# Block products in the down projections: five weight slots of eleven worked as seven products with summed weights in place of eight

## The chip, the cores and the metric

One core of one Trainium2 chip. The number reported is the device time of one execution in microseconds. The core has four compute engines that run their own instruction queues and meet at semaphores: TensorE (PE), VectorE (DVE), ScalarE (ACT) and GpSimd (POOL). SyncE (SP) issues the DMAs.

## What is computed

Two transformer-like blocks over 256 tokens of width 1024, all in float32. Four times in it stands a gated feed-forward of this form, with the inner width F = 2816:

```python
def swiglu_ffn(h, w13, w2):
    gate, up = jnp.split(h @ w13, 2, axis=-1)
    return (jax.nn.silu(gate) * up) @ w2      # (256, 2816) @ (2816, 1024)

x = x + 0.5 * swiglu_ffn(rms_norm(x, ffn1_norm[l]), ffn1_w13[l], ffn1_w2[l])   # ffn 0; ffn 1 alike
h = h + swiglu(rms_norm_2(h, ln_ffn[i]), ffn_w_in[i], ffn_w_out[i])            # ffn 2 and 3
```

Between them stand a convolution and attention mixer (after ffn 0), a gated delta rule mixer (after ffn 1, with the first block's final norm ahead of it), a gated embedding and a stick-breaking attention (after ffn 2), and a gated embedding at the end (after ffn 3). The change is in the products with `w2` and `ffn_w_out`, the down projections `down0` to `down3`.

## The kernel before

**Precision.** TensorE works in its rounded float32. Each float32 matrix is split into a rounded part and the rest (`whi`, `wlo` for weights, `hThi`, `hTlo` for the hidden state, `xThi`, `xTlo` for the input of other products), and each product is three matmuls, hi by hi, hi by lo and lo by hi (`passes`, L1717 to L1719). One such matmul has 128 rows of contraction, 128 tokens and 512 columns.

**The ring of weights.** All weights stream through one list of slots of 128x2048 float32 (1 MB). SP loads slot w into `raw[w % 4]` once slot w-4 is wholly split (L422, L423). ACT rounds it into `whi[w % 4]` once TensorE has used slot w-4 (`split`, L457). VectorE subtracts, `wlo = raw - whi` (L1112, or in two halves, L1109 and L1112, for a few slots). TensorE waits for `w_lo` and counts up `w_used` when it is done with a slot. ACT and VectorE each go through their queues in program order; `split(n)` means "go on through slot n-1", so a written order decides what else stands between two splits.

**A down projection** is 11 slots (`wide`). A slot holds two blocks of 128 rows of the weight and its 1024 columns, and is worked for both tiles of 128 tokens: 2 token tiles by 2 row blocks by 2 halves of 512 columns, 8 block products, 24 matmuls. The sums stay in four PSUM banks (6, 7, 2, 3). The first seven slots are taken one after the other; the last four are first worked for token tile 0 and then for tile 1, so that tile 0 comes out early. Ahead of the last quarter of tile 1 stand the transposes of the next stage's first token tile (`turn_T`, L1751).

**What follows a down.** VectorE adds the banks to the residual `X` (`residual`, L1158), ACT sums squares (L481), GpSimd takes the root (L1001, L1002), VectorE scales (L1127), TensorE transposes (L1751), ACT and VectorE split the result into `xThi`, `xTlo` (L488, L1135), and the next stage's products begin. VectorE splits the next slots of the ring in between.

**What goes into a down.** The hidden state of each of the 11 blocks is transposed in 32x32 pieces by VectorE (L1176), written to memory and read back by DMA (L406, L413), and split by ACT and VectorE (`hidden_hi` L513, `hidden_lo` L1168). Blocks 8, 9 and 10 are split while the down runs.

## Time and profile before

| | |
|---|---|
| median of 3 runs | 1212.18 us (1209.71 to 1213.11) |
| the profiled execution | 1209.79 us, span 1208.1 us |
| granted TensorE clock | 1.00 of full in every slice |
| busy: PE, DVE, ACT, POOL | 1191.5, 786.5, 610.5, 80.1 us |
| first down projection | 133.25 to 193.99 us of the span |

The busy time of an engine is over the whole span. Matmuls are pipelined and their records overlap, so the distance between starts is their pace, not the duration of one. The remaining 1.7 us of the profiled time lie around the span.

### The profile page before, as it was taken

Reading aid. Unit: us, or ns where it says so; the run is one execution under the profiler, and the core shown is the slowest. Engines: PE = TensorE matmul, PEld = TensorE weight load, DVE = VectorE, ACT = ScalarE, POOL = GpSimd, SP = SyncE. Lnnn points to the kernel's source line nnn. Section 1 sums busy time; section 2 is a strip of 40 time slices with the busy share of each in tenths; the row PEclk is TensorE's granted clock in tenths of the full one; section 3 lists DMA queues with packets and bytes.
Section 4 is the critical chain, followed back from the end, with each engine's and each line's share of the span. In section 5 each row is a group of like instructions: output and inputs, shape, how many; then the busy total and the mean of one; then the engine's idle time right before and its main releaser. Section 6 shows DMA issues by size and latency. Waiting matters only on the chain.

```text
span 1208.1 us, 16080 instructions
## 1 busy us (share of the span) xinstructions
PE 1191.5 (99%) x6352; PEld 1011.9 (84%) x6352; DVE 786.5 (65%) x941; ACT 610.5 (51%) x770; POOL 80.1 (7%) x151
## 2 busy tenths in 40 slices
PE   8999999999999999999999999999999999999998
PEld 6888888988888888899898888888888888888886
DVE  4766547997665654788877756553688666565545
ACT  5544426565544443565644544543556755445333
POOL 1000003001000000400002000000114000000000
PEclk9999999999999999999999999999999999999999
DMA  8987764552588775545203688686355347877630
GB/s 272 318 279 250 236 217 147 160 192 59 177 271 244 243 243 175 193 157 174 88 1 105 193 274 256 218 255 211 136 206 202 131 129 233 259 257 230 227 136 36
DMA packets 174547, 235.32 MB, mean 195 GB/s; under 512 B 13993, under 2 KB 131849, under 8 KB 174473
## 3 DMA queue, kind: packets, MB, share of 16 engines
q1 hardware_dynamic: 174472, 234.30, 60.0%
q8 instruction: 50, 0.82, 0.3%
q14 instruction: 25, 0.20, 0.0%
HBM read 221.67 MB, written 12.58 MB: 194 GB/s over the span
## 4 chain that ended last, share of the span: by engine, by line
PE 93%; DVE 4%; ACT 1%; POOL 1%; DMA 0%; issue 0%; SPq 0%; DVEq 0%; ACTq 0%
PE bank L1717 28%; PE bank L1718 28%; PE bank L1719 28%; PE bank L1751 1%; PE bank L2146 1%; PE bank L2163 1%; PE bank L2171 1%; DMA raw<-in_ffn_w_dram 0%; PE bank L1970 0%; DVE xs L1523 0%; DVE bv L1378 0%; PE bank L2268 0%; DVE xs L1127 0%; PE bank L2290 0%; PE bank L1957 0%
## 5 line engine op out<-in xcount | busy, mean ns | idle before, releaser
L1112 DVE TENSOR_TENSOR wlo<-raw,whi 128x2048 fp32r<-128x2048 f32 (+1 forms) x190 | 415.9, 2194 | 236.4 <-ACT whi L457 236.4
L457 ACT ACTIVATE whi<-raw 128x2048 fp32r<-128x2048 f32 x190 | 362.9, 1914 | 227.2 <-PE bank L1719 218.4
L1717 PE MATMUL bank<-whi,xThi 128*128 128x512 f32 x1024 | 401.8, 392 | 0.9 <-DVE xTlo L1659 0.8
L1719 PE MATMUL bank<-whi,xTlo 128*128 128x512 f32 x1024 | 398.9, 390 | 0.0
L1718 PE MATMUL bank<-wlo,xThi 128*128 128x512 f32 x1024 | 398.5, 389 | 0.0
L1717 PEld LDWEIGHTS bank<-whi,xThi 128*128 128x128 f32 x1024 | 192.3, 188 | 41.4 <-DVE xTlo L1659 1.4
L1719 PEld LDWEIGHTS bank<-whi,xTlo 128*128 128x128 f32 x1024 | 192.2, 188 | 40.3
L1718 PEld LDWEIGHTS bank<-wlo,xThi 128*128 128x128 f32 x1024 | 192.3, 188 | 38.8
L1717 PE MATMUL bank<-whi,hThi 128*128 128x512 f32 x352 | 137.3, 390 | 0.0
L1719 PE MATMUL bank<-whi,hTlo 128*128 128x512 f32 x352 | 137.0, 389 | 0.0
L1718 PE MATMUL bank<-wlo,hThi 128*128 128x512 f32 x352 | 136.9, 389 | 0.0
L541 ACT ACTIVATE hnat<-bank 128x256 f32<-128x256 f32 x88 | 33.6, 384 | 122.3 <-PE bank L1719 122.3
L1717 PE MATMUL bank<-xThi,whi 128*128 128x256 f32 x288 | 82.3, 286 | 0.0
L1718 PE MATMUL bank<-xTlo,whi 128*128 128x256 f32 x288 | 81.5, 283 | 0.0
L1719 PE MATMUL bank<-xThi,wlo 128*128 128x256 f32 x288 | 81.4, 283 | 0.0
L1719 PEld LDWEIGHTS bank<-whi,hTlo 128*128 128x128 f32 x352 | 66.1, 188 | 13.7
L1717 PEld LDWEIGHTS bank<-whi,hThi 128*128 128x128 f32 x352 | 66.1, 188 | 13.7
L1718 PEld LDWEIGHTS bank<-wlo,hThi 128*128 128x128 f32 x352 | 66.1, 188 | 13.5
L1001 POOL TENSOR_SCALAR meansq<-sumsq 128x1 f32<-128x1 f32 x16 | 12.4, 773 | 841.0 <-ACT xs L481 665.1
L1193 DVE TENSOR_TENSOR hnat<-hnat,bank 128x256 f32<-128x256 f32 x88 | 36.7, 417 | 45.8 <-ACT hnat L541 45.8
L1717 PEld LDWEIGHTS bank<-xThi,whi 128*128 128x128 f32 x288 | 55.2, 192 | 1.3 <-issue 0.8
L1718 PEld LDWEIGHTS bank<-xTlo,whi 128*128 128x128 f32 x288 | 55.2, 192 | 0.0
(425 smaller groups left out, 1064.3 us busy)
## 6 DMA issues: line engine op xcount, KB each, us to landing
raw<-in_ffn_w_dram SPq DMA_DIRECT2D x176, 256.0 KB, 4.5
raw<-in_ffn_w_in_dram SPq DMA_DIRECT2D x176, 256.0 KB, 4.0
raw<-in_ffn_w_dram SPq DMA_DIRECT2D x22, 1024.0 KB, 5.3
raw<-in_ffn_w_out_dram SPq DMA_DIRECT2D x22, 1024.0 KB, 5.4
raw<-in_gdn_w_in_dram SPq DMA_DIRECT2D x16, 1024.0 KB, 5.5
hidden<-hblk SPq DMA_DIRECT2D x44, 256.0 KB, 5.1
hraw<-hidden SPq DMA_DIRECT2D x176, 64.0 KB, 3.3
raw<-in_ple_w_gate_dram SPq DMA_DIRECT2D x8, 1024.0 KB, 5.0
```

The costliest lines, as they stand in the source:

```text
L457: act.activation(whi[w % SPLIT][:], raw[w % RAW][:], ACT.Copy).then_inc(w_hi, 1)
L541: act.activation(hnat[:, j % 2, t, :], bank[2 * (j % 2) + t][:, 0:256], ACT.Silu).then_inc(sem("ffn_silu"), 1)
L1001: step(pool.tensor_scalar(meansq[:, c], sumsq[:, 2 * n + t, 0:1], sumsq[:, 2 * n + t, 1:2], EPS, ALU.add, ALU.add))
L1112: dve.tensor_tensor(wlo[w % SPLIT][:, c], raw[w % RAW][:, c], whi[w % SPLIT][:, c].bitcast(F32), ALU.subtract).then_inc(w_lo, 1)
L1193: dve.tensor_tensor(hnat[:, j % 2, t, :], hnat[:, j % 2, t, :], bank[2 * (j % 2) + t][:, 256:512], ALU.mult).then_inc(sem("ffn_h"), 1)
L1717: pe.matmul(psum, lhs[0], rhs[0], start=start, stop=False, skip_group_check=True)
L1718: pe.matmul(psum, lhs[0], rhs[1], start=False, stop=False, skip_group_check=True)
L1719: return pe.matmul(psum, lhs[1], rhs[0], start=False, stop=stop, skip_group_check=True)
L1751: ins = pe.transpose(bank[4 + b][:, k * P:(k + 1) * P], xs[:, t, (4 * b + k) * P:(4 * b + k + 1) * P], ident[:])
L2146: ins = pe.matmul(bank[q][:, h * P:(h + 1) * P], A_[q][:, h, :], T[q][:, h, :], start=True, stop=True)
L2163: ins = pe.matmul(bank[q][:, c], U[q][:, h, :], Y[q][:, c], start=True, stop=True)
L2171: ins = pe.matmul(psum[:, h * P:(h + 1) * P], lhs(h), rhs(h), start=True, stop=True)
```

## The change

Five slots of each down (row block pairs 1, 2, 4, 5 and 6) are worked as 2x2 block matrices by seven products in place of eight. For that each of them takes two places of the ring: its own, with the quarters b0, b1 (first row block, left and right half of the columns), b2, b3 (second row block), 128x512 each, and behind it a place without a DMA, which holds four sums of quarters: GpSimd computes t0 = b0-b1 and t1 = b0-b2 in one instruction (`first_combined`), VectorE t2 = b2-t0 and then t3 = b3-t2, which waits for it (`combine`). Of the first place only three quarters are rounded and split; the second is rounded and split whole. On the side of the hidden state GpSimd adds hi and lo back together (`h_all`) and forms four sums S1 to S4 of it (`hidden_sums`), which ACT rounds (`sums_hi`) and VectorE splits (`sums_lo`) into the buffers of `xThi` and `xTlo`, free while a down runs. Each of the five takes 21 matmuls in place of 24. The products go to seven banks in all; four of these hold parts that belong to more than one output quarter, and after the last split of a down VectorE adds them to `X` with 4+3+2+2 instructions (`shared_sums`), ahead of the adds of `residual`. A down is now 16 places of the ring, of which five have no DMA. `wide` passes over the second place of each pair and calls `seven` for the first.

The diff, cut; what is left out are the names of buffers and the calls that pass `pair_at`:

```diff
+
+    def stream_down(name, w):
+        first[name] = len(slots)
+        v = w.rearrange("(k p) n -> p k n", p=P)
+        for s in range(KF // 2):
+            slots.append([(("rows", 2), v[:, 2 * s:2 * s + 2, :])])
+            if s in SEVEN:
+                slots.append([])
+
     stream_gate_up("up0", a["ffn1_w13"][0])
-    stream_wide("down0", a["ffn1_w2"][0])
+    stream_down("down0", a["ffn1_w2"][0])
     stream_pairs("mix", a["w_in"][0])
...
 
 
     WIDE = ["down0", "mix_out", "down1", "gdn_out", "down2", "ple_g0", "sb_out", "down3", "ple_g1"]
-    wide_slots = {n: (KF if n[:4] == "down" else KD) // 2 for n in WIDE}
+    wide_slots = {n: KF // 2 + len(SEVEN) if n[:4] == "down" else KD // 2 for n in WIDE}
+    pair_at = {s + sum(x < s for x in SEVEN): s for s in range(KF // 2)}
+    seven_at = {s + sum(x < s for x in SEVEN): m for m, s in enumerate(SEVEN)}
+    SEVEN_SLOTS = [first[f"down{f}"] + i for f in range(4) for i in sorted(seven_at)]
+    COMBINED = [w + 1 for w in SEVEN_SLOTS]
 
 
...
+        S1, S2, S3, S4 = range(4)
+        sum_hi, sum_lo = (x[:].rearrange("p (m a) (b c) -> p m (a b) c", a=2, c=P) for x in (xThi, xTlo))
...
+                    if w in COMBINED:
+                        act.wait_ge(sem("seven_w"), COMBINED.index(w) + 1)
                     if w >= SPLIT:
                         act.wait_ge(w_used, w - SPLIT + 1)
-                    act.activation(whi[w % SPLIT][:], raw[w % RAW][:], ACT.Copy).then_inc(w_hi, 1)
+                    c = slice(512 if w in SEVEN_SLOTS else 0, SLOT)
+                    act.activation(whi[w % SPLIT][:, c], raw[w % RAW][:, c], ACT.Copy).then_inc(w_hi, 1)
                     split_to[0] += 1
 
...
+
+                def sums_hi(m):
+                    act.wait_ge(sem("seven_sum"), len(SEVEN) * f + m + 1)
+                    if m >= 4:
+                        act.wait_ge(w_used, SEVEN_SLOTS[len(SEVEN) * f + m - 4] + 2)
+                    act.activation(sum_hi[:, m % 4], h_sum[:, m % 2], ACT.Copy).then_inc(sem("seven_hi"), 1)
+                act.wait_ge(w_used, first[f"down{f}"])
+                sums_hi(0)
+                sums_hi(1)
                 split(first[f"down{f}"] + SPLIT + 2)
                 hidden_hi(NBLK - 2)
+                sums_hi(2)
+                sums_hi(3)
                 split(first[f"down{f}"] + SPLIT + 4)
                 hidden_hi(NBLK - 1)
+                for m in range(4, len(SEVEN)):
+                    sums_hi(m)
 
             def mixer1():
                 s = first["mix"]
...
 
+            def first_combined(n):
+                w = SEVEN_SLOTS[n]
+                pool.wait_ge(raw_in[w % RAW], arrived[w])
+                pool.wait_ge(w_lo, split_done(w + 1 - RAW))
+                b = raw[w % RAW][:].rearrange("p (q c) -> p q c", q=4)
+                t = raw[(w + 1) % RAW][:].rearrange("p (q c) -> p q c", q=4)
+                pool.tensor_tensor(t[:, 0:2], b[:, 0:1].broadcast_to([P, 2, 512]), b[:, 1:3], ALU.subtract).then_inc(sem("seven_t"), 1)
+
+            def hidden_sums(f):
+                for m, s in enumerate(SEVEN):
+                    n = len(SEVEN) * f + m
+                    if m == 2:
+                        first_combined(n - 2)
+                    if m >= 2:
+                        first_combined(n - 1)
+                    pool.wait_ge(sem("ffn_lo"), NBLK * f + s + 1)
+                    if n:
+                        pool.wait_ge(sem("seven_sum"), n)
+                    step(pool.tensor_tensor(h_all[:], hThi[:, s].bitcast(F32), hTlo[:, s].bitcast(F32), ALU.add))
+                    if n >= 2:
+                        pool.wait_ge(sem("seven_lo"), n - 1)
+                    v = h_sum[:, m % 2]
+                    pool.tensor_tensor(v[:, S3], h_all[:, 2], h_all[:, 0], ALU.subtract)
+                    step(pool.tensor_tensor(v[:, S1], h_all[:, 2], h_all[:, 3], ALU.add))
+                    step(pool.tensor_tensor(v[:, S2], v[:, S1], h_all[:, 0], ALU.subtract))
+                    pool.tensor_tensor(v[:, S4], h_all[:, 1], v[:, S2], ALU.subtract).then_inc(sem("seven_sum"), 1)
+                first_combined(len(SEVEN) * f + len(SEVEN) - 1)
...
 
+            def combine(w):
+                dve.wait_ge(sem("seven_t"), SEVEN_SLOTS.index(w) + 1)
+                b = raw[w % RAW][:].rearrange("p (q c) -> p q c", q=4)
+                t = raw[(w + 1) % RAW][:].rearrange("p (q c) -> p q c", q=4)
+                step(dve.tensor_tensor(t[:, 2], b[:, 2], t[:, 0], ALU.subtract))
+                dve.tensor_tensor(t[:, 3], b[:, 3], t[:, 2], ALU.subtract).then_inc(sem("seven_w"), 1)
+
             def split(n):
 
                 while split_to[0] < min(n, NSLOT):
                     w = split_to[0]
+                    if w in SEVEN_SLOTS:
+                        combine(w)
                     dve.wait_ge(w_hi, split_done(w))
                     if w in HALVED:
                         c = slice(0, SLOT // 2)
                         dve.tensor_tensor(wlo[w % SPLIT][:, c], raw[w % RAW][:, c], whi[w % SPLIT][:, c].bitcast(F32),
                                           ALU.subtract).then_inc(w_half, 1)
-                    c = slice(SLOT // 2 if w in HALVED else 0, SLOT)
+                    c = slice(SLOT // 2 if w in HALVED else 512 if w in SEVEN_SLOTS else 0, SLOT)
                     dve.tensor_tensor(wlo[w % SPLIT][:, c], raw[w % RAW][:, c], whi[w % SPLIT][:, c].bitcast(F32),
...
                 split(last_group(name) + SPLIT)
+                if name[:4] == "down":
+                    shared_sums(last_group(name), scale)
                 return add
+
+            def shared_sums(done, scale):
+
+                def into(product, *quarters):
+                    for t, h in quarters:
+                        c = slice(h * 512, (h + 1) * 512)
+                        ins = dve.scalar_tensor_tensor(out=X[:, t, c], in0=product[:], scalar=scale, in1=X[:, t, c],
+                                                       op0=ALU.mult, op1=ALU.add)
+                    step(ins)
+                dve.wait_ge(w_used, done)
+                into(bank[4], (0, 1), (0, 0), (1, 1), (1, 0))
+                into(bank[0], (0, 0), (1, 1), (1, 0))
+                into(bank[5], (0, 0), (1, 0))
+                into(bank[1], (1, 1), (1, 0))
 
             def ffn(f):
...
                         setup()
+
+                def sums_lo(m):
+                    dve.wait_ge(sem("seven_hi"), len(SEVEN) * f + m + 1)
+                    dve.tensor_tensor(sum_lo[:, m % 4], h_sum[:, m % 2], sum_hi[:, m % 4].bitcast(F32), ALU.subtract).then_inc(sem("seven_lo"), 1)
+                sums_lo(0)
+                sums_lo(1)
                 split(first[f"down{f}"] + SPLIT + 2)
                 hidden_lo(NBLK - 2)
+                sums_lo(2)
+                sums_lo(3)
                 split(first[f"down{f}"] + SPLIT + 4)
                 hidden_lo(NBLK - 1)
+                for m in range(4, len(SEVEN)):
+                    sums_lo(m)
 
             def setup():
 
...
 
+            def seven(f, i):
+                w, m, s = first[f"down{f}"] + i, seven_at[i], pair_at[i]
+                begins = m == 0
+
+                def product(psum, lhs, at, rhs, fresh):
+                    return passes(psum[:], lhs, [x[:, 512 * rhs:512 * rhs + 512] for x in at], fresh, False)
+
+                def hidden(t, k):
+                    return [x[:, s, 2 * t + k, :] for x in hT]
+
+                def combined(q):
+                    return [x[:, m % 4, q, :] for x in (sum_hi, sum_lo)]
+                pe.wait_ge(w_lo, split_done(w))
+                pe.wait_ge(sem("ffn_lo"), NBLK * f + s + 1)
+                if begins:
+                    pe.wait_ge(sem("ffn_h"), 2 * (NBLK * f + NBLK - 1) + 2)
+                product(bank[4], hidden(0, 0), ring(w), 1, begins)
+                product(bank[7], hidden(0, 1), ring(w), 3, False)
+                pe.wait_ge(sem("seven_lo"), len(SEVEN) * f + m + 1)
+                product(bank[6], combined(S4), ring(w), 2, False).then_inc(w_used, 1)
+                pe.wait_ge(w_lo, split_done(w + 1))
+                product(bank[5], combined(S1), ring(w + 1), 0, begins)
+                product(bank[1], combined(S3), ring(w + 1), 1, begins)
+                product(bank[0], combined(S2), ring(w + 1), 2, begins)
+                product(bank[3], hidden(1, 1), ring(w + 1), 3, False).then_inc(w_used, 1)
```

## Rows read from the trace of the kernel before

**Rows 1.** The page: busy times, chain that ended last, costliest groups.

```profile
PE 1191.5 (99%) x6352; PEld 1011.9 (84%) x6352; DVE 786.5 (65%) x941; ACT 610.5 (51%) x770; POOL 80.1 (7%) x151
...
PE 93%; DVE 4%; ACT 1%; POOL 1%; DMA 0%; issue 0%; SPq 0%; DVEq 0%; ACTq 0%
...
L1717 PE MATMUL bank<-whi,hThi 128*128 128x512 f32 x352 | 137.3, 390 | 0.0
```

**Rows 2.** Timeline of TensorE, first down: start, duration, engine, line, tiles, count.

```profile
133.25 0.39 PE L1717 MATMUL bank<-whi,hThi 128*128 128x512 f32 x1
...
190.38 1.03 PE L1751 MATMUL bank<-ident,xs 128*128 128x128 f32 x8
...
193.99 0.39 PE L1717 MATMUL bank<-whi,xThi 128*128 128x512 f32 x1
...
198.07 1.04 PE L1751 MATMUL bank<-ident,xs 128*128 128x128 f32 x8
```

**Rows 3.** Timeline of ScalarE, first down; in brackets idle before, releaser.

```profile
138.95 1.92 ACT L457 ACTIVATE whi<-raw 128x2048 fp32r<-128x2048 f32 x1 [2.79 <-PE bank L1719]
```

**Rows 4.** Timeline of VectorE, start of the first down.

```profile
135.68 2.29 DVE L1112 TENSOR_TENSOR wlo<-raw,whi 128x2048 fp32r<-128x2048 f32 x1 [1.38 <-ACT whi L457]
...
138.52 0.65 DVE L1168 TENSOR_TENSOR hTlo<-hraw,hThi 128x512 fp32r<-128x512 f32 x1
...
140.90 2.29 DVE L1112 TENSOR_TENSOR wlo<-raw,whi 128x2048 fp32r<-128x2048 f32 x1 [1.74 <-ACT whi L457]
...
146.34 2.29 DVE L1112 TENSOR_TENSOR wlo<-raw,whi 128x2048 fp32r<-128x2048 f32 x1 [3.15 <-ACT whi L457]
```

**Rows 5.** DMA issues by line: count, size, median microseconds from issue to landing.

```profile
raw<-in_ffn_w_dram SPq DMA_DIRECT2D x22, 1024.0 KB, 5.3
```

**Rows 6.** Timeline of GpSimd and VectorE after the second down.

```profile
475.85 0.69 DVE L1158 SCALAR_TENSOR_TENSOR X<-bank,X 128x512 f32<-128x512 f32 x1 [5.22 <-PE bank L1719]
...
481.91 1.42 DVE L1127 SCALAR_TENSOR_TENSOR xs<-X,rstd,gain 128x512 f32<-128x512 f32 x2 [1.07 <-POOL rstd L1035]
...
494.20 2.20 DVE L1127 SCALAR_TENSOR_TENSOR xs<-X,rstd,gain 128x512 f32<-128x512 f32 x2 [1.07 <-POOL rstd L1035]
...
494.65 1.20 POOL L1042 TENSOR_TENSOR rows_of<-ones 64x512 fp32r<-64x512 f32 x1
```

**Rows 7.** Timeline of GpSimd and VectorE, three later places.

```profile
640.71 0.69 DVE L1516 TENSOR_TENSOR dec<-bv,u 128x512 f32<-128x512 f32 x1
...
640.22 1.66 POOL L992 TENSOR_TENSOR ors<-oms,half 128x8 f32<-128x8 f32 x1
...
849.13 0.30 POOL L1001 TENSOR_SCALAR meansq<-sumsq 128x1 f32<-128x1 f32 x1 [173.35 <-ACT xs L481]
...
860.00 1.22 DVE L1109 TENSOR_TENSOR wlo<-raw,whi 128x1024 fp32r<-128x1024 f32 x1
...
861.13 1.22 DVE L1112 TENSOR_TENSOR wlo<-raw,whi 128x1024 fp32r<-128x1024 f32 x1
...
860.93 1.50 POOL L1001 TENSOR_SCALAR meansq<-sumsq 128x1 f32<-128x1 f32 x1 [10.85 <-ACT xs L481]
```

**Rows 8.** Timeline of VectorE, end of the first down.

```profile
173.54 2.29 DVE L1112 TENSOR_TENSOR wlo<-raw,whi 128x2048 fp32r<-128x2048 f32 x1 [3.15 <-ACT whi L457]
...
181.06 0.69 DVE L1158 SCALAR_TENSOR_TENSOR X<-bank,X 128x512 f32<-128x512 f32 x1 [5.22 <-PE bank L1719]
...
184.95 1.42 DVE L1127 SCALAR_TENSOR_TENSOR xs<-X,rstd,gain 128x512 f32<-128x512 f32 x2 [1.85 <-POOL rstd L1002]
...
187.14 2.29 DVE L1112 TENSOR_TENSOR wlo<-raw,whi 128x2048 fp32r<-128x2048 f32 x1 [0.78 <-ACT whi L457]
...
192.14 1.28 DVE L1135 TENSOR_TENSOR xTlo<-bank,xThi 128x512 fp32r<-128x512 f32 x2
...
194.19 0.69 DVE L1158 SCALAR_TENSOR_TENSOR X<-bank,X 128x512 f32<-128x512 f32 x1 [0.17 <-PE bank L1719]
```

More of the change, by code:

```diff
@@ L82, in stream_wide @@
             slots.append([(("rows", 2), v[:, 2 * s:2 * s + 2, :])])
+    SEVEN = (1, 2, 4, 5, 6)
+    def stream_down(name, w):
[5 more added lines that the diff above has]
+                slots.append([])
     stream_gate_up("up0", a["ffn1_w13"][0])
-    stream_wide("down0", a["ffn1_w2"][0])
+    stream_down("down0", a["ffn1_w2"][0])
     stream_pairs("mix", a["w_in"][0])
@@ L90, in build_program @@
     stream_gate_up("up1", a["ffn2_w13"][0])
-    stream_wide("down1", a["ffn2_w2"][0])
+    stream_down("down1", a["ffn2_w2"][0])
     stream_blocks("gdn", a["gdn_w_in_2"][0], (6, 0, 1, 2, 3, 4, 5, 7))
@@ L94, in build_program @@
     stream_gate_up("up2", a["ffn_w_in_2"][0], 0)
-    stream_wide("down2", a["ffn_w_out_2"][0])
+    stream_down("down2", a["ffn_w_out_2"][0])
     stream_wide("ple_g0", a["ple_w_gate_2"][0])
@@ L101, in build_program @@
     stream_gate_up("up3", a["ffn_w_in_2"][1], 1)
-    stream_wide("down3", a["ffn_w_out_2"][1])
+    stream_down("down3", a["ffn_w_out_2"][1])
     stream_wide("ple_g1", a["ple_w_gate_2"][1])
@@ L208, in build_program @@
             gate_s = lent.enter_context(nc.sbuf_tensor("gate_s", [P, NT, D], F32))
-        hThi, hTlo, hnat, hblk, hraw, p_in, pThi, pTlo, pp, row_tap, row_tap4 = region(
+        hThi, hTlo, hnat, hblk, hraw, h_all, h_sum, p_in, pThi, pTlo, pp, row_tap, row_tap4 = region(
             [("hThi", [P, NBLK, 4, P], F32R), ("hTlo", [P, NBLK, 4, P], F32R),
-             ("hnat", [P, 2, NT, 256], F32), ("hblk", [P, 2, 4, P], F32), ("hraw", [P, 2, 4, P], F32)],
+             ("hnat", [P, 2, NT, 256], F32), ("hblk", [P, 2, 4, P], F32), ("hraw", [P, 2, 4, P], F32),
+             ("h_all", [P, 4, P], F32), ("h_sum", [P, 2, 4, P], F32)],
             [("p_in", [P, NT, PLE], F32), ("pThi", [P, 2, SEQ], F32R), ("pTlo", [P, 2, SEQ], F32R),
@@ L1079, in mixer3 @@
                             root(krs[:, i, t, h], kms[:, i, t, h], kss[:, i, t, h], P, ("s_kss", "s_krs"), 4 * i + 2 * b + t + 1)
+            def first_combined(n):
[24 more added lines that the diff above has]
+                first_combined(len(SEVEN) * f + len(SEVEN) - 1)
             norm(0)
+            hidden_sums(0)
             mixer1()
             norm(2)
+            hidden_sums(1)
             mixer2()
             norm(5)
+            hidden_sums(2)
             norm(6)
@@ L1088, in _ @@
             norm(9)
+            hidden_sums(3)
             norm(10)
@@ L1764, in wide @@
                 for i, t in order:
+                    if src is hT and i not in pair_at:
+                        continue
+                    if src is hT and i in seven_at:
+                        if t == 0:
+                            seven(int(name[4:]), i)
+                        continue
                     if t == 0:
@@ L1767, in wide @@
                         if ready:
-                            ready(i)
+                            ready(pair_at[i] if src is hT else i)
                     if ready_t:
@@ L1775, in wide @@
                         middle()
-                    k0 = 2 * (pairs[i] if pairs else i)
+                    k0 = 2 * (pairs[i] if pairs else pair_at[i] if src is hT else i)
                     ins = rows(s + i, t, src, k0, 2, [out_bank(t, 0), out_bank(t, 1)], i == 0, i == n - 1,
```

## The prediction

> **What bounds the kernel now.** I read the page first. TensorE is busy in 99% of the span and holds 93% of the chain that ended last [rows 1]; the reader is to see that a matmul less is a gain only as long as no other engine makes TensorE wait. Then the timeline of TensorE in the first down: 252 matmuls of 512 columns from 133.25 to 190.38, so one every 0.2267 us, and a slot of 24 in 5.44 us [rows 2]. The page has 352 of each of the three passes for four downs, 88 x 3 = 264 per down [rows 1]. Last the timelines of ScalarE and VectorE, which bring the slots. ScalarE rounds one in 1.92 us after it idled 2.79 us for TensorE to free the ring [rows 3], VectorE subtracts in 2.2 us and then idles 3.15 us [rows 4]. So a slot costs VectorE 2.2 us of TensorE's 5.44: it has 3 us per slot to give, and the change asks for them.
>
> **The gain.** 20 slots lose 3 matmuls each: 60 x 0.2267 = 13.6 us, 3.4 per down. TensorE would then need a pair of places (21 matmuls) every 4.76 us, 9 matmuls (2.04 us) for the first place and 12 (2.72) for the second.
>
> **What VectorE and GpSimd get.** I place events by the first down, positions 0 to 15 of the ring, with TensorE starting at 133.25. Prices from rows: a 128x512 subtraction with both inputs in SBUF 0.65 [rows 4], so a whole split 2.2, three quarters of one 1.65, `combine` 2 x 0.65 plus about 0.1 for the wait between them = 1.4, `sums_lo` 0.65. ScalarE: 1.9 whole, 1.45 for three quarters, 0.6 for `sums_hi`. GpSimd has one row of an elementwise two-input instruction of size: 512 elements in 1.20 us [rows 6], so 2.3 for the 1024 elements of `first_combined` (estimate), 1.2 for `h_all`, 0.36 for each of the four 128-element sums, 2.8 for a `hidden_sums` block with its waits. Positions 0 to 3 and the first two blocks of sums are made while the up projection still runs, and there is room there: VectorE's splits of positions 2 and 3 end where they did, at 132.2 and 137.5 to 137.9 (the longer `combine` is paid by the shorter split). At 138.5 it has `hidden_lo` as before [rows 4], at 139 it starts on what the seven products need: five `sums_lo` (3.3), whole splits at 4, 5, 7, 9, 11 (11.0), short ones at 6, 8, 10 (5.0), three `combine` (4.2), two `hidden_lo` (1.3): 24.8 us up to position 11. TensorE wants position 11 at 133.25 + 5.44 + 4.76 x 2 + 5.44 + 4.76 x 2 + 2.04 = 165.2. So VectorE has 26 us for 24.8 of its own work, before any wait.
>
> **Two engines, one after the other.** In the same 26 us GpSimd has the sums of block 4 (their second half 1.6), `first_combined` at 6, 8 and 10 (6.9), and the blocks 5 and 6 (5.6): 14.1 us. Do these lie beside VectorE's? [rows 6] show two pairs of `xs<-X,rstd,gain`, both inputs in SBUF: 1.42 us alone, 2.20 with a GpSimd subtraction of 1.20 us from 494.65 to 495.85 beside it; the second half ended 0.7 us late, as if it had begun when GpSimd ended. [rows 7] show the reverse: a root's first step on GpSimd, 0.30 us otherwise, took 1.50 beside two subtractions of VectorE and ended after the second, though that one was issued later than it. So neither runs while the other reads two operands, and GpSimd gets in only where VectorE pauses. Then the two sums add: 24.8 + 14.1 = 39 us where 26 are there. Played through in program order it is a little more, as each needs the other: the sums of block 4 wait for the splits of 4 and 5 (to 145.3) and `hidden_lo`, end at 146.8; `first_combined` of 6 to 149.1; block 5's sums to 152.5, because `sums_lo` got in between; `first_combined` of 8 to 154.8; `combine` of 6 to 157.9 with `h_all` between its two halves; split of 6 to 159.6, where TensorE wanted it at 153.7. Position 7 is split at 162.4, `first_combined` of 10 waits for its DMA (5.3 us after the split of 6, [rows 5]) and ends at 167.2, 8 is split at 171.0, 9 at 173.5, 10 at 176.6, 11 at 179.1. TensorE gets to 11 at 179.2, not 165: a stall of 14 us per down, the largest pieces ahead of positions 6 and 8, about 6 us each. The bound from below is the bare sum, 13.
>
> How long an operation holds the other engine decides this price. [rows 7] have a case against the full duration: beside a power on GpSimd over 8 elements, 1.66 us long, VectorE's two-input product took its 0.69. The Trainium skill, SBUF — State Buffer, section Who interferes with whom, says that such a pair excludes each other for the whole instruction; by it all 14.1 us count. By the row only the reading part does; start and end of 17 instructions, about 0.1 each, would drop out, 1.7 us per down and 7 in all. I keep the full sum, since the streaming subtraction of [rows 6] held VectorE to its end, and leave the 7 us to the range.
>
> **The end of a down.** `shared_sums` is 11 instructions like L1158, 0.69 alone and 0.65 in a row, with four waits: 7.7 us. They stand between the last split and the first add, where VectorE idled 5.22 us [rows 8]; the two adds then need no wait between them, which gives 0.7 back. That makes the scaling 1.8 us late; when the last slots come late (their DMA is issued only when 11 is split) another 2.1. TensorE's next stage has the first transposes with 0.1 to spare after that. VectorE's queue from there holds two slots' splits, `turn_lo` at 192.14 and the add at 194.19 [rows 8], with 1.2 us of idle time in all; `turn_lo` comes 2.7 late against 1.3 of lead over the mixer's first matmul at 193.99 [rows 2]: 1.4 us lost, and 1.0 more at the transposes of the second token tile, which had no lead at all at 198.07 [rows 2]. That is 2.4 for the first down; for the third and fourth, where those transposes come later, 1.4; for the second, where two norms stand in the chain (from the add at 475.85 to the scaling at 481.91, 6.1 us in place of 3.9, [rows 6]), I take 4.0. Together 9.2 us; 2 if the slots come in time.
>
> Cost at nothing: ScalarE's ten pieces more per down (five roundings of sums and five of second places, about 10 us of 60, beside 2.8 idle per slot [rows 3]); the missing DMAs, since the bytes are the same; the read-back of the hidden blocks, due only in the last group. Were ScalarE's cover gone, `sums_hi` would cost its 0.6 each, 12 us in all. The first two `first_combined` and two blocks of sums per down (10 us of GpSimd in the up projection) fall in VectorE's idle time there.
>
> **Sum.** Per down -3.4 + 14.0 = 10.6, four times 42.4, plus 9.2 = 51.6 us. On the profiled execution, 1209.8, that is 1261.4; it lies 2.4 below the median, so I predict 1263.8 for the median, say 1264.
>
> **Rivals.** (1) The two engines run side by side. Then the chain is bound by VectorE's own 24.8 us and its waits for GpSimd: played through without exclusion, position 11 comes 1.7 us late, and the end of a down costs the 9.2. 4 x (1.7 - 3.4) + 9.2 = +2.4: 1214.6, no change. For it: GpSimd's power did not hold VectorE. Against it: [rows 6] and the first step in [rows 7].
> (2) The other side, faster: slots come in time, as the exclusive sum stays under 26 us; that needs GpSimd's part under 1.3 us, or no exclusion and two-input instructions there at half my price. From there on the gain of 13.6 shows, less 2 at the ends: 1200.6. Against it: the row of 1.20 us for 512 elements.
> (3) TensorE's clock falls in the stalls. The trace of before has it at full, 2.4 GHz, throughout, and TensorE never idle for long, so no row shows a fall. If it went to 1.2 GHz at the two long waits of a down, 21 matmuls of a pair would take 4.8 us more; the first time this hides in the next wait, the second time not: 4.4 to 9 us per down, 1282 to 1300. The Trainium skill, TensorE: Matmul & The Clock Gate, Part 1, has the clock at half after idleness; no row here can confirm it.
> That the change does little because the products are few can't be: the matmuls go whatever the waits do.
>
> **Chances.** Forecast (exclusion) 0.60, between 1235 (GpSimd's sums a third cheaper) and 1282; rival 1 0.18, 1204 to 1222; rival 2 0.12; rival 3 0.10. The range goes down to rival 1's 1204 and up to 1290, which leaves out rival 2 and part of rival 3. A measurement of this kernel can tell about 0.3%, 3.6 us, from no change. Faster: rival 2 and a bit of rival 1, 0.14; same 0.11 of rival 1; slower 0.75.
>
> **What would show it.** Right: in each down two gaps on TensorE of about 6 us, ahead of positions 6 and 8, released by VectorE; a down of about 72 us in place of 60.7; GpSimd's `first_combined` or sums with durations well over 2.3 and 0.36 where VectorE subtracts, and VectorE's subtractions of 0.65 stretched where GpSimd is on; transposes after a down late. Wrong: a down of 57 to 59 us, GpSimd's durations at their bare price beside a busy VectorE. The price of GpSimd's instructions, taken from one row over half the partitions, is what I trust least; next, who gets in first when both wait.

## The result and the profile after

The changed kernel takes 1253.36 us (median of 4 runs, 1250.85 to 1255.27) against 1211.76 of the kernel before beside it (median of 4). The ratio is 1.034, with a 95% interval of 1.032 to 1.037: 42 us slower, where 1264 was predicted, in the range of 1204 to 1290. The profiled executions lie 45.4 us apart by their spans, 1253.5 against 1208.1: that of the changed kernel is 1.9 us above its median, that of before 2.0 below its own. Terms read from the traces are held against the 45.4.

The page of the changed kernel, its busy times, its chain that ended last and two of the costliest groups:

```profile
PE 1197.8 (96%) x6292; PEld 1011.5 (81%) x6292; DVE 930.9 (74%) x1065; ACT 649.0 (52%) x810; POOL 249.2 (20%) x271
...
PE 71%; DVE 12%; POOL 6%; issue 5%; ACT 3%; DMA 2%; SPq 0%; POOLq 0%; DVEq 0%; ACTq 0%
...
L1121 POOL TENSOR_TENSOR raw<-raw 128x1024 f32<-128x1024 f32 x20 | 60.1, 3007 | 188.7 <-DMA raw<-in_ffn_w_out_dram 102.6
...
L1133 POOL TENSOR_TENSOR h_all<-hThi,hTlo 128x512 f32<-128x512 f32 x20 | 30.3, 1516 | 211.0 <-DVE hTlo L1259 211.0
```

TensorE's share of the chain fell from 93% [rows 1] to 71%; VectorE and GpSimd stand there with 12% and 6%. TensorE's waits over the whole span, grouped by what ended them (total, times, longest, in us):

```profile
PE bank L1818 <- DVE wlo L1187: 33.4, 8, 5.6
PE bank L1818 <- DVE xTlo L1210: 5.3, 4, 1.7
```

Eight waits, two in each down, 33.4 us, all for a split of VectorE; and one at each start of a next stage, 5.3 us. TensorE's timeline in the first down, which answers to [rows 2]:

```profile
133.80 0.39 PE L1818 MATMUL bank<-whi,hThi 128*128 128x512 f32 x1
...
153.97 0.39 PE L1820 MATMUL bank<-whi,hTlo 128*128 128x512 f32 x1
159.97 0.80 PE L1818 MATMUL bank<-whi,hThi 128*128 128x512 f32 x1 [5.61 <-DVE wlo L1187]
160.56 0.63 PE L1819 MATMUL bank<-wlo,hThi 128*128 128x512 f32 x1
160.99 0.63 PE L1820 MATMUL bank<-whi,hTlo 128*128 128x512 f32 x1
...
166.25 0.39 PE L1820 MATMUL bank<-whi,hTlo 128*128 128x512 f32 x1
169.32 0.50 PE L1818 MATMUL bank<-whi,hThi 128*128 128x512 f32 x1 [2.69 <-DVE wlo L1187]
...
172.60 0.63 PE L1818 MATMUL bank<-whi,xThi 128*128 128x512 f32 x1
...
175.83 0.39 PE L1818 MATMUL bank<-whi,hThi 128*128 128x512 f32 x1
...
177.87 0.39 PE L1818 MATMUL bank<-whi,xThi 128*128 128x512 f32 x1
...
203.01 0.39 PE L1820 MATMUL bank<-whi,hTlo 128*128 128x512 f32 x1
204.13 0.50 PE L1818 MATMUL bank<-whi,xThi 128*128 128x512 f32 x1 [0.73 <-DVE xTlo L1210]
```

The start at 133.80 and the last matmul at 203.01 are 69.2 us apart, 60.5 before (133.25 to 193.76, one pace ahead of the row at 193.99). The waits stand ahead of positions 6 (159.97) and 8 (169.32). The rows at 172.60, 175.83 and 177.87 are the starts of positions 9, 10 and 11. Behind each of the two waits some seven matmuls come every 0.43 us in place of 0.227. Added up from the starts, the two waits cost 8.6 us of this down and the slow matmuls 3.4.

VectorE in the same down, which answers to [rows 4] and [rows 8]; L1295 is `sums_lo`, L1172 and L1173 are `combine`, L1187 a split, L1259 `hidden_lo`, L1246 `shared_sums`:

```profile
138.96 1.28 DVE L1295 TENSOR_TENSOR xTlo<-h_sum,xThi 128x512 fp32r<-128x512 f32 x2
141.47 4.76 DVE L1187 TENSOR_TENSOR wlo<-raw,whi 128x2048 fp32r<-128x2048 f32 x2 [1.24 <-ACT whi L478]
146.16 2.88 DVE L1259 TENSOR_TENSOR hTlo<-hraw,hThi 128x512 fp32r<-128x512 f32 x1
148.96 1.78 DVE L1295 TENSOR_TENSOR xTlo<-h_sum,xThi 128x512 fp32r<-128x512 f32 x1
153.25 2.20 DVE L1295 TENSOR_TENSOR xTlo<-h_sum,xThi 128x512 fp32r<-128x512 f32 x1 [2.52 <-ACT xThi L576]
155.38 1.75 DVE L1172 TENSOR_TENSOR raw<-raw 128x512 f32<-128x512 f32 x1
...
157.91 4.47 DVE L1187 TENSOR_TENSOR wlo<-raw,whi 128x1536 fp32r<-128x1536 f32 x2
...
165.33 6.14 DVE L1187 TENSOR_TENSOR wlo<-raw,whi 128x1536 fp32r<-128x1536 f32 x2
...
172.72 1.75 DVE L1187 TENSOR_TENSOR wlo<-raw,whi 128x1536 fp32r<-128x1536 f32 x1
174.83 4.49 DVE L1187 TENSOR_TENSOR wlo<-raw,whi 128x2048 fp32r<-128x2048 f32 x2 [0.36 <-ACT whi L478]
...
185.15 2.29 DVE L1187 TENSOR_TENSOR wlo<-raw,whi 128x2048 fp32r<-128x2048 f32 x1 [0.67 <-ACT whi L478]
187.36 7.04 DVE L1246 SCALAR_TENSOR_TENSOR X<-bank,X 128x512 f32<-128x512 f32 x11
194.44 1.29 DVE L1233 SCALAR_TENSOR_TENSOR X<-bank,X 128x512 f32<-128x512 f32 x2
...
203.40 1.28 DVE L1210 TENSOR_TENSOR xTlo<-bank,xThi 128x512 fp32r<-128x512 f32 x2
```

A row of two splits (x2) is given the form of its first: those at 157.91 and 165.33 are a short split and the whole one behind it, positions 6 and 7 and positions 8 and 9. The rows at 172.72 and 174.83 bring 10, and 11 with 12.

And GpSimd, which before had nothing to do here; L1121 is `first_combined`, L1133 `h_all`, L1137 to L1140 the four sums:

```profile
113.25 2.41 POOL L1121 TENSOR_TENSOR raw<-raw 128x1024 f32<-128x1024 f32 x1 [33.29 <-DMA raw<-in_ffn_w_dram]
...
141.60 2.49 POOL L1140 TENSOR_TENSOR h_sum<-h_all,h_sum 128x128 f32<-128x128 f32 x1
144.05 4.44 POOL L1121 TENSOR_TENSOR raw<-raw 128x1024 f32<-128x1024 f32 x1
148.45 1.74 POOL L1133 TENSOR_TENSOR h_all<-hThi,hTlo 128x512 f32<-128x512 f32 x1
...
152.09 0.46 POOL L1140 TENSOR_TENSOR h_sum<-h_all,h_sum 128x128 f32<-128x128 f32 x1
...
160.31 2.39 POOL L1140 TENSOR_TENSOR h_sum<-h_all,h_sum 128x128 f32<-128x128 f32 x1
165.19 2.47 POOL L1121 TENSOR_TENSOR raw<-raw 128x1024 f32<-128x1024 f32 x1 [2.49 <-DMA raw<-in_ffn_w_dram]
```

The reader is to compare durations of one form. The subtraction of L1121 is 2.41 us at 113.25, where it starts while VectorE pauses (the split that VectorE issues beside it, at 114.46, takes 3.34 in place of 2.29), and 4.44 at 144.05, where it began beside VectorE's splits of 141.47 to 146.2. VectorE's `hidden_lo` right behind them is 2.88 in place of 0.65, and ends at 149.04, 0.55 after the end of GpSimd's subtraction at 148.49. L1140 is 0.46 alone and 2.49 or 2.39 beside a split. And the two splits at 141.47 took 4.76 us in place of 2 x 2.2, 0.36 more, as if that L1140 had had its turn between them: it was issued at 141.60, behind the first split's start, and ended at 144.09, about its own 0.46 after the first split's end. In these rows the two engines take turns.

### The profile page after: what moved, and what is told of

It is laid out like the page before. It is cut to its first block, busy times and chain, and to the rows that moved or that the text cites. A ratio compares the mean times of both kernels' runs of the same rounds, so it can differ in the third digit from the quotient of the medians.

```text
span 1253.5 us, 16343 instructions
## 1 busy us (share of the span) xinstructions
PE 1197.8 (96%) x6292; PEld 1011.5 (81%) x6292; DVE 930.9 (74%) x1065; ACT 649.0 (52%) x810; POOL 249.2 (20%) x271
## 4 chain that ended last, share of the span: by engine, by line
PE 71%; DVE 12%; POOL 6%; issue 5%; ACT 3%; DMA 2%; SPq 0%; POOLq 0%; DVEq 0%; ACTq 0%
PE bank L1818 21%; PE bank L1819 21%; PE bank L1820 21%; DVE wlo L1187 4%; DVE X L1246 2%; POOL h_sum L1140 2%; DMA raw<-in_ffn_w_dram 1%; ACT whi L478 1%; POOL h_all L1133 1%; DMA raw<-in_ffn_w_out_dram 1%; PE bank L1852 1%; PE bank L2279 1%; POOL h_sum L1139 1%; PE bank L2296 1%; POOL h_sum L1137 1%
## 5 line engine op out<-in xcount | busy, mean ns | idle before, releaser
L1187 DVE TENSOR_TENSOR wlo<-raw,whi 128x2048 fp32r<-128x2048 f32 (+2 forms) x210 | 462.3, 2211 | 152.6 <-ACT whi L478 152.1
L478 ACT ACTIVATE whi<-raw 128x2048 fp32r<-128x2048 f32 (+1 forms) x210 | 391.3, 1872 | 185.2 <-PE bank L1820 130.5
L1818 PE MATMUL bank<-whi,xThi 128*128 128x512 f32 x1104 | 437.0, 396 | 6.5 <-DVE xTlo L1210 5.3
L1819 PE MATMUL bank<-wlo,xThi 128*128 128x512 f32 x1104 | 432.2, 391 | 0.0
L1820 PE MATMUL bank<-whi,xTlo 128*128 128x512 f32 x1104 | 431.9, 391 | 0.0
L1818 PE MATMUL bank<-whi,hThi 128*128 128x512 f32 x252 | 102.1, 405 | 33.4 <-DVE wlo L1187 33.4
L1820 PE MATMUL bank<-whi,hTlo 128*128 128x512 f32 x252 | 101.4, 402 | 0.0
L1819 PE MATMUL bank<-wlo,hThi 128*128 128x512 f32 x252 | 100.9, 400 | 0.0
L1121 POOL TENSOR_TENSOR raw<-raw 128x1024 f32<-128x1024 f32 x20 | 60.1, 3007 | 188.7 <-DMA raw<-in_ffn_w_out_dram 102.6
L1133 POOL TENSOR_TENSOR h_all<-hThi,hTlo 128x512 f32<-128x512 f32 x20 | 30.3, 1516 | 211.0 <-DVE hTlo L1259 211.0
```

The lines of the kernel that those rows point to most:

```text
L478: act.activation(whi[w % SPLIT][:, c], raw[w % RAW][:, c], ACT.Copy).then_inc(w_hi, 1)
L1121: pool.tensor_tensor(t[:, 0:2], b[:, 0:1].broadcast_to([P, 2, 512]), b[:, 1:3], ALU.subtract).then_inc(sem("seven_t"), 1)
L1133: step(pool.tensor_tensor(h_all[:], hThi[:, s].bitcast(F32), hTlo[:, s].bitcast(F32), ALU.add))
L1187: dve.tensor_tensor(wlo[w % SPLIT][:, c], raw[w % RAW][:, c], whi[w % SPLIT][:, c].bitcast(F32), ALU.subtract).then_inc(w_lo, 1)
L1818: pe.matmul(psum, lhs[0], rhs[0], start=start, stop=False, skip_group_check=True)
L1819: pe.matmul(psum, lhs[0], rhs[1], start=False, stop=False, skip_group_check=True)
```

## The experiments

**1. GpSimd as busy, but reading nothing.** Its sums become fills of the same tiles.

```diff
-                pool.tensor_tensor(t[:, 0:2], b[:, 0:1].broadcast_to([P, 2, 512]), b[:, 1:3], ALU.subtract).then_inc(sem("seven_t"), 1)
+                step(pool.memset(t[:, 0:2], 0.0))
+                step(pool.memset(t[:, 0:1], 0.0))
+                pool.memset(t[:, 0:2], 0.0).then_inc(sem("seven_t"), 1)
...
-                    step(pool.tensor_tensor(h_all[:], hThi[:, s].bitcast(F32), hTlo[:, s].bitcast(F32), ALU.add))
+                    step(pool.memset(h_all[:], 0.0))
+                    step(pool.memset(h_all[:], 0.0))
```

and two fills of 128x128 for each of the four sums.

> GpSimd's subtractions and additions for the sums are replaced by fills of the same tiles, two or three for each, so that GpSimd is busy about as long (2.4, 1.1 and 0.4 us) but reads nothing; its output is left out, the sums are zero. Exclusion theory (GpSimd and VectorE block each other while both read two operands): the two long waits of TensorE per down (8.35 us) and the half clock behind them (about 3.8) nearly vanish, 1205 to 1215 us. Rival, late results (TensorE waits because the sums come through a chain of queues that takes its time, whatever the ports do): within 5 us of the changed kernel, 1248 to 1258.

Measured: 1212.11 us, ratio 1.0006 (0.9997 to 1.0016): 41 of the 42 us are gone. The waits of TensorE, and the busy times of the engines in the 26 us in which the forecast had counted (in this view: the stretch, its length, busy us and instructions of PE, PEld, DVE, ACT, POOL, granted clock):

```profile
PE bank L1825 <- DVE wlo L1194: 4.2, 12, 0.6
PE bank L1825 <- DVE xTlo L1217: 4.1, 4, 1.7
PE bank L1859 <- DVE xs L1209: 2.3, 3, 0.8
```

```profile
139.00:165.00 26.00, 25.39 (x110) 20.10 (x109) 22.02 (x21) 16.75 (x14) 14.05 (x37) 1.00 0.51 166
```

VectorE was busy 22.0 us and GpSimd 14.05 in the same 26 us, side by side, 36 us of work in all. In the changed kernel the same stretch shows:

```profile
139.00:165.00 26.00, 20.39 (x83) 16.47 (x82) 21.93 (x16) 11.44 (x10) 22.29 (x16) 0.87 0.30 101
158.00:162.00 4.00, 2.03 (x5) 1.66 (x6) 3.90 (x2) 2.43 (x2) 3.84 (x3) 0.50 0.23 19
170.00:174.00 4.00, 4.00 (x12) 3.10 (x11) 3.96 (x4) 1.12 (x1) 0.00 (x0) 0.57 0.83 303
```

21.9 and 22.3 us, and yet less done: these busy times hold the time in which one engine waited inside its instruction for the other. Busy time alone does not show such a wait; the duration of one form against another place does. The other two lines are for the clock, below. The rival of this run, that GpSimd's results merely come too late for TensorE, whatever it reads, is refuted.

**2. All sums on VectorE.** `first_combined` and `hidden_sums` leave GpSimd; `combine` makes all four weight sums, and VectorE the sums of the hidden state, two blocks in the up projection and three in the down.

```diff
-                dve.wait_ge(sem("seven_t"), SEVEN_SLOTS.index(w) + 1)
+                dve.wait_ge(raw_in[w % RAW], arrived[w])
+                dve.wait_ge(w_lo, split_done(w + 1 - RAW))
...
+                step(dve.tensor_tensor(t[:, 0:2], b[:, 0:1].broadcast_to([P, 2, 512]), b[:, 1:3], ALU.subtract))
                 step(dve.tensor_tensor(t[:, 2], b[:, 2], t[:, 0], ALU.subtract))
...
                 sums_lo(1)
+                dve.wait_ge(sem("seven_lo"), len(SEVEN) * f + 2)
+                sums(2)
+                sums(3)
```

> All sums of weights and of the hidden state on VectorE, none on GpSimd. Exclusion theory: VectorE's work up to position 11 becomes about 34 us in place of 25 + 14 one after the other, so 3 to 4 us less per down: 1236 to 1243. Rival, side by side (VectorE only waits for GpSimd's results, their work overlaps): 9 us more of VectorE's work per down with nothing taken from its path, 1265 to 1290.

Measured: 1243.92 us, 1.026 (1.025 to 1.028), 9.4 us faster than the changed kernel although VectorE has more to do. That is 0.9 above the range that I had expected for exclusion, and 21 below that for side by side. Taking an engine away made it faster: what GpSimd took over cost VectorE more, in turns, than doing it itself.

**3. About half of GpSimd's reading.** The weight sums are real, the sums of the hidden state are the fills of experiment 1.

```diff
-                    step(pool.tensor_tensor(h_all[:], hThi[:, s].bitcast(F32), hTlo[:, s].bitcast(F32), ALU.add))
+                    step(pool.memset(h_all[:], 0.0))
+                    step(pool.memset(h_all[:], 0.0))
...
-                    pool.tensor_tensor(v[:, S3], h_all[:, 2], h_all[:, 0], ALU.subtract)
...
+                    step(pool.memset(v[:, S3], 0.0))
+                    pool.memset(v[:, S3], 0.0)
```

> GpSimd really subtracts the weights (three times 2.4 us per down in TensorE's window), but fills in place of the sums of the hidden state, about as long as they are (the output lacks them). Exclusion as a sum: of the 41 us between the run with fills only and the changed kernel this brings back the share of the reading time, about 7.2 of 15.6 us, 19 us: 1226 to 1236. Rival, one of the two kinds alone makes the wait: 1210 to 1216 or 1248 to 1256.

Measured: 1233.09 us, 1.018 (1.017 to 1.020). 21.0 of the 41.3 us between the run of fills and the changed kernel are back, 19 were expected. The price goes about with the time for which GpSimd reads.

**4. Without the shared adds.**

```diff
                 split(last_group(name) + SPLIT)
-                if name[:4] == "down":
-                    shared_sums(last_group(name), scale)
                 return add
```

> Without the 11 adds of the shared products to the residual after a down (they are left out). Forecast's step: they make the end of a down late, 7 us of VectorE's queue of which 5.2 were idle before, 7 to 8 us in all over four downs: 1244 to 1248. Rival, hidden in VectorE's idle time of the last group: 1251 to 1255.

Measured: 1244.26 us, 1.027 (1.025 to 1.029), 9.1 us less than with them, a little more than expected. The 5.3 us of waits for `xTlo` at the next stages are gone from its trace.

**5. The clock kept up.**

```diff
+                for i in range({2: 22, 3: 8}.get(m, 0)):
+                    pe.matmul(bank[7][:], hThi[:, 0, 0, :], hThi[:, 0].rearrange("p m c -> p (m c)"), start=False, stop=False, skip_group_check=True)
                 pe.wait_ge(w_lo, split_done(w))
```

> 22 matmuls that nobody needs ahead of the wait at position 6 and 8 ahead of that at position 8, on data that lies ready (they are added into one output bank, so the output is changed). They fit into the waits of 5.6 and 2.7 us. Clock theory (the half clock after each long wait costs TensorE about 3.8 us per down): the granted clock stays 1.00 and the time falls by 10 to 16 us, 1238 to 1244. Rival, supply alone sets the pace: the clock stays up and the time is the same within 4 us, 1250 to 1257.

Measured: 1254.93 us (1251.15 to 1257.99), 1.035 (1.033 to 1.038), as the changed kernel. Its clock in the same places:

```profile
158.00:162.00 4.00, 3.20 (x14) 2.01 (x12) 3.90 (x3) 2.01 (x2) 3.92 (x2) 1.00 0.36 63
170.00:174.00 4.00, 4.00 (x13) 3.10 (x11) 3.97 (x4) 1.58 (x1) 0.00 (x0) 0.61 0.92 348
```

Behind the first wait it stayed at 1.00 (0.50 in the changed kernel), behind the second it fell all the same in three of the four downs (0.61 in the first, against 0.57). The waits shrank from 33.4 to 11.6 us and the first down took 69.4 us (133.26 to 202.67) against 69.2. The rival holds for the first fall: its slow matmuls only filled time in which TensorE would have waited. What the second costs is read from the downs of one kernel in which it did or did not come. In the kernel of experiment 4 it came in the first down and in no other; the same four us behind the second wait, in the first and the third down:

```profile
170.20:174.20 4.00, 4.00 (x12) 3.09 (x11) 3.96 (x4) 1.12 (x1) 0.00 (x0) 0.57 0.85 308
851.80:855.80 4.00, 4.00 (x19) 3.08 (x18) 3.96 (x4) 1.14 (x1) 0.00 (x0) 1.00 0.84 297
```

Position 12 started 46.80 us after the down's start with the fall, and 46.26, 46.30 and 46.53 without it; in `keep_clock` 46.88 and 46.63. So the second fall costs 0.25 to 0.55 us per down, 1 to 2 us in all: most of its slow matmuls too fall into time in which the splits of 9, 10 and 11 would have held TensorE up.

**6. Eight products in place of seven, with all sums.** A product more for each pair, into a bank where it is not wanted:

```diff
+                product(bank[2], hidden(1, 0), ring(w + 1), 3, False)
                 product(bank[3], hidden(1, 1), ring(w + 1), 3, False).then_inc(w_used, 1)
```

> The changed kernel with all its sums, but with three more matmuls in each of the 20 pairs, so 24 again (the extra product is added into an output bank, the output is changed). Supply theory: ahead of positions 6 and 8 TensorE waits anyway, so the three pairs before the second wait take their extra matmuls for nothing, and only the last two pairs of a down show them, 2 x 0.68 x 4 = 5.4 us: 1256 to 1261. Rival, matmuls count wherever they stand: 60 x 0.2267 = 13.6 us more, 1265 to 1269.

Measured: 1253.64 us (1253.00 to 1254.83), 1.035 (1.034 to 1.037). Not even the 5 us of the last two pairs show: for the time, 60 matmuls, 13.6 us of TensorE's, weigh nothing. They came in below the range that I had expected, for two reasons. At full clock VectorE's splits set the pace up to position 11 (the third down of experiment 4 started 9, 10 and 11 within 0.1 us of the ends of their splits), so matmuls ahead of 11 fill waits. And with the second wait shorter (1.36 us in the first down) the clock did not fall behind it:

```profile
170.00:174.00 4.00, 4.00 (x18) 3.08 (x18) 3.96 (x4) 0.67 (x1) 0.00 (x0) 1.00 0.73 255
```

Position 12 started 46.99 us after the down's start, against 46.79 in the changed kernel with the fall and 46.26 without one in experiment 4. So the three matmuls of the last pair do cost their 0.7 us, and the clock gave most of that back: this run alone does not show that they are free.

**7. Fills, and no shared adds.** The kernel of experiment 1 with the edit of experiment 4:

```diff
-                if name[:4] == "down":
-                    shared_sums(last_group(name), scale)
```

> GpSimd fills in place of summing (reads nothing) and the adds of the shared products left out as well; the output lacks both. If the two costs, exclusion and the adds at the end of a down, are all that stands against the gain, what is left is 60 matmuls fewer, 13.6 us, less the waits of under 0.5 us each seen with the fills (4.2 us in all): 1198 to 1203. Rival, something else in the 16-place ring costs too (fewer places in flight, later DMAs): 1205 or more.

Measured: 1205.32 us, 0.996 (0.994 to 0.997), above what I expected. In its trace the downs take 58.8, 58.9, 58.6 and 59.4 us, where 57.1 would be the pure gain (60.5 less 3.4). Waits of about 0.3 us for splits remain (nine, 3.2 us); with their starts and gaps too short for that list, TensorE's starts lie 6.7 us further apart in the four downs than in those of before. VectorE's own queue has no time to spare even if GpSimd costs it nothing. Of the gain of 13.6 us some 7 stay out of reach for five pairs worked in this order (4 x 58.9 against 4 x 57.1), however cheap GpSimd's part.

**8 and 9. Two pairs only, with the shared adds early or late.** Pairs 1 and 2, whose sums are ready before the down begins. `two_early` has the adds after position 4, `two_late` where the change has them.

```diff
-    SEVEN = (1, 2, 4, 5, 6)
+    SEVEN = (1, 2)
...
-                for m in range(4, len(SEVEN)):
-                    sums_lo(m)
+                shared_sums(first[f"down{f}"] + 5, 0.5 if f < 2 else 1.0)
```

> Seven products only for the row block pairs 1 and 2, whose sums are all made while the up projection runs, and the 11 shared adds right after their products, in VectorE's idle time of the plain slots. 24 matmuls fewer: 5.4 us. No exclusion falls on TensorE's path and nothing is late at the end of a down: 1205 to 1208. Rival, the second places of the ring or the adds in mid-down still cost: 1210 or more.

> The same two pairs with the shared adds where the change has them, after the last split. Against two_early it shows the price of their place alone, without late slots: by the forecast 2 us (slots in time), by the run with GpSimd's fills, whose waits for the next stage's input came to about 6 us, 5 to 7: 1208 to 1213. Rival, the place does not matter: as two_early within 1 us.

Measured: 1205.36 us, 0.995 (0.994 to 0.997), against 1210.25 before: faster, by 4.9 us where 5.4 is the pure gain. Its downs take 59.15 us, 1.36 less than before, six matmuls to the digit. Late: 1206.35 us, 0.996 (0.995 to 0.998). The two runs overlap, so the place of the adds costs at most 1 to 2 us when the last slots come in time; in the trace it is one wait of 0.5 us at the second down's end and about as much behind it. That is below the 5 to 7 that I expected here and the 2 of the prediction; the rival of this run, within 1 us of `two_early`, holds.

**10. Three pairs, all on VectorE, adds early.** On the kernel of experiment 2:

```diff
-    SEVEN = (1, 2, 4, 5, 6)
+    SEVEN = (1, 2, 5)
...
-                if name[:4] == "down":
-                    shared_sums(last_group(name), scale)
...
+                split(first[f"down{f}"] + 12)
+                shared_sums(first[f"down{f}"] + 9, 0.5 if f < 2 else 1.0)
```

> Pairs 1, 2 and 5, all sums on VectorE (GpSimd has none), shared adds after the third pair's products. 36 matmuls fewer: 8.2 us. VectorE has about 36 us of work from the down's start to the first add, where 41 are there: no wait, 1203 to 1206. Rival, VectorE's queue gets late at the third pair or its adds hold up the last splits: 1207 to 1215.

Measured: 1204.89 us, 0.996 (0.995 to 0.997). The downs take 59.5 us where 58.5 would be the pure gain: waits of 0.2 us near positions 1 and 12.

**11. Three pairs, mixed.** GpSimd makes what falls into the up projection, VectorE the third pair's weight sums, and the shared adds go in two lumps between the last splits.

```diff
+                if m < 2:
+                    dve.wait_ge(sem("seven_t"), 2 * f + m + 1)
+                else:
+                    dve.wait_ge(raw_in[w % RAW], arrived[w])
+                    dve.wait_ge(w_lo, split_done(w + 1 - RAW))
+                    step(dve.tensor_tensor(t[:, 0:2], b[:, 0:1].broadcast_to([P, 2, 512]), b[:, 1:3], ALU.subtract))
...
+                split(first[f"down{f}"] + 12)
+                scale = 0.5 if f < 2 else 1.0
+                shared_sums(first[f"down{f}"] + 9, scale, 0)
+                split(first[f"down{f}"] + 12 + 1)
+                shared_sums(first[f"down{f}"] + 9, scale, 1)
```

> Pairs 1, 2 and 5. GpSimd makes the first two weight sums, in the up projection, and the hidden sums, of which the third block's second half (1.8 us) falls in the down; VectorE makes the third pair's weight sums itself; the shared adds go in two lumps, 7 and 4 instructions, between the last splits. Against the run with three pairs wholly on VectorE the small waits (1.0 us per down) should go: 1201 to 1204. Rival, the waits come from VectorE's load at the third pair, wherever the rest stands: 1204 to 1207.

Measured: 1201.18 us, 0.992 (0.991 to 0.994), against 1211.57 before. This one beats both kernels, that of before by 9 us going by the ratio (10 between the medians) and the changed one by 52. VectorE at the end of its first down, with the adds (L1245) between splits and idle time left ahead of the first add of the residual (L1234), as in [rows 8]:

```profile
161.31 4.49 DVE L1188 TENSOR_TENSOR wlo<-raw,whi 128x2048 fp32r<-128x2048 f32 x2 [2.95 <-ACT whi L478]
165.72 4.40 DVE L1245 SCALAR_TENSOR_TENSOR X<-bank,X 128x512 f32<-128x512 f32 x7
170.16 2.29 DVE L1188 TENSOR_TENSOR wlo<-raw,whi 128x2048 fp32r<-128x2048 f32 x1
172.37 2.60 DVE L1245 SCALAR_TENSOR_TENSOR X<-bank,X 128x512 f32<-128x512 f32 x4
175.01 2.29 DVE L1188 TENSOR_TENSOR wlo<-raw,whi 128x2048 fp32r<-128x2048 f32 x1
179.04 0.69 DVE L1234 SCALAR_TENSOR_TENSOR X<-bank,X 128x512 f32<-128x512 f32 x1 [1.74 <-PE bank L1823]
```

And TensorE's first matmul of that down and of the mixer behind it, which answer to 133.25 and 193.99 in [rows 2]:

```profile
133.26 0.39 PE L1821 MATMUL bank<-whi,hThi 128*128 128x512 f32 x1
...
191.98 0.39 PE L1821 MATMUL bank<-whi,xThi 128*128 128x512 f32 x1
```

58.7 us from the one to the other against 60.7: nine matmuls fewer (2.04 us), and nothing given back. Over four downs that is 8.2 us; the interval of the ratio is 7.6 to 10.9 us.

## Why the prediction was right

**The gain, 3.4 us per down.** Right as a count of matmuls, and right that it would not show: experiment 6 puts it at nothing. Where supply allows it, it is there in full (experiments 8 and 11).

**Exclusion.** The mechanism was right and is shown by experiment 1: take away the reading and keep GpSimd busy, and 41 us vanish. Experiments 2 and 3 agree in size. The positions of the two waits were right too, 6 and 8, and the length of the first; the second was 2.7 us and not about 6. The split of 6 was put at 159.6 and that of 7 at 162.4; TensorE went on at 159.97, and the two splits of 157.91 ended at 162.38.

**Its size, 14.0 us per down, was 1.4 to 1.9 too high.** The downs took 69.2 to 69.7 us, 8.7 to 9.2 more than before, so the supply cost 12.1 to 12.6 with the 3.4 added back. Two things were off. Position 8: I had put `first_combined` of 10 ahead of `combine` of 8. Its DMA landed at 165.2, about when I had it (164.9), but by then that `combine` (164.00 to 165.41) was all but done. So 8 was split at 169.3, not at 171.0, and 9 to 11 came earlier with it: their splits ended at 171.5, 174.5 and 177.1, and TensorE, slowed by the clock, came to them only at 172.60, 175.83 and 177.87. And the turns: from [rows 7] I had it that GpSimd gets in only where VectorE pauses. In this down an instruction of GpSimd that stood waiting got the next turn between two queued ones of VectorE (144.05 against `hidden_lo` at 146.16). Why the root's step of [rows 7], issued at 860.93, had to let a second subtraction of 861.13 go first is open. GpSimd's bare prices were a little higher than taken, 2.41, 1.30 and 0.46 us for 2.3, 1.2 and 0.36, which worked the other way.

By the rule of the Trainium skill (SBUF — State Buffer, Who interferes with whom) a VectorE instruction with two inputs in SBUF and a GpSimd instruction that reads SBUF exclude each other, for the whole length of the one that came first; in this trace the streaming subtractions did, in both directions, as in [rows 6], so it counts as a whole. Of the 0.1 us at start and end that I had put in doubt, about that much did drop out (`first_combined` of 144.05 ended 2.26 behind the end of the splits, with a bare price of 2.41), but the bare prices were 0.1 higher than I had taken them, and the two cancel.

**The end of a down, 9.2 us in all.** Right in the sum, with some luck in the parts: the first down lost less than the 2.4 that I had put there, the second more than its 4.0. Measured about 9.5 in the traces: next stages 0.9, 1.8, 1.4 and 1.8 us later than the downs themselves, and 3.5 more behind the second down, where two norms stand in the chain. Leaving out the adds gave 9.1 back. For slots that come in time the forecast was 2, and experiments 8 and 9 show about 1. With the 35.4 us of the downs and half a microsecond ahead of the first this is the whole difference of 45.4.

**What was to hide things hid them.** In the downs every wait of TensorE that is listed was for VectorE, none for ScalarE.

**The rivals.** (1) Side by side: 1214.6 was its time, and experiment 1, which makes it true, gave 1212.1; it was the right price for a wrong premise. (2) The faster side needed the exclusive sum under 26 us; experiment 7 shows that for five pairs it would not have been met even then: 1205 and not 1200.6. (3) The clock did fall, to 0.50 of full behind the first long wait and 0.57 behind the second, where I had given it one chance in ten. The Trainium skill, TensorE: Matmul & The Clock Gate, Part 1, has the clock at half after idleness, and this trace agrees. But the price that I had worked out, 4.4 to 9 us per down, did not show. Each fall held for some seven matmuls and not for 21; experiment 5 kept the clock up behind the first wait for no gain; and the second fall cost 0.25 to 0.55 us per down, since splits of VectorE set the pace behind the second wait as well. The forecast had no term for the clock, so in the 12.1 to 12.6 us of a down these 0.25 to 0.55 are the clock's.

## What to carry to other kernels

Before work is moved to a second engine, ask whether the two can run at once: two-input work in SBUF on GpSimd came out of VectorE's time, nearly for its full length, and the same work in VectorE's idle stretches cost nothing. A saving on the engine that is busy 99% is worth only as much as the slack of the one that feeds it; count that engine's work per piece, with the new work, against the new and shorter piece. Then take only as much of the saving as the slack pays for: three pairs gave 9 us where five cost 42.

## What the hardware showed that I had not expected

GpSimd's two-input instructions on float32 took 0.46, 1.30 and 2.41 us for 128, 512 and 1024 elements per partition, about 2.2 ns per element and 0.18 us besides. Fills took 0.53 and 0.96 us for 512 and 1024 and did not touch VectorE: its two splits in a row took 4.49 us beside them, as in a place where GpSimd is idle. A power on GpSimd over 8 elements did not hold VectorE [rows 7], a subtraction did, but for about the last 0.1 us. TensorE's granted clock fell after both long waits of a down: it was 0.50 of full, 1.2 GHz, in the stretch from 158 to 162 behind 5.6 us of waiting, and 0.57 in that from 170 to 174 behind 2.7 us, where the matmuls up to 173.4 came at the pace of 1.2 GHz. A wait of about 2.1 us did not settle it: in `keep_clock` the clock fell behind three such waits (0.61 in the first down) and stayed at 1.00 behind the fourth. In the run of fills, with twelve waits of at most 0.6 us for splits, it was 1.00 in the same 26 us.
